# Gate and up strips as pairs in seven block products, activations through DRAM between up and down

## The chip, the cores and the metric

The kernel runs on one core of one Trainium2 chip. TensorE (PE in the profile) multiplies, and its weight loads are shown as PEld; VectorE is DVE, ScalarE is ACT, GpSimd is POOL, and SyncE (SP) issues nearly all DMAs. PSUM is TensorE's output memory, eight banks of 512 float32 values in each of 128 partitions; SBUF is the memory in which all else is kept on the core; DRAM is the memory outside it. The metric is the device time in microseconds; several runs of a kernel give a median. The profile is one execution of its own.

## The reference

Two layers over 1024 tokens of width 1024, all in float32. Layer 0 mixes with RWKV-7, layer 1 with forgetting attention over shared keys and values; both attend to a memory of 256 rows, and each ends with the part that is changed here:

```
x = x + concat([main_out, mem_out]) @ w_out[l]
h = rms_norm(x, ffn_norm[l])
gu = h @ w_gate_up                       # 1024 -> 2 * 2816
x = x + (silu(gu[:, :2816]) * gu[:, 2816:]) @ w_down      # 2816 -> 1024
```

Between the layers the shared keys and values (`w_kv`) and layer 1's input (`b_w_in`) are projected, with an RMS norm per head on keys and queries.

## The kernel before, in words

The stream X lies transposed in SBUF, features on partitions: 8 tiles k of 128 features by 1024 tokens. A projection is a sequence of **strips**: 128 output columns of a weight, 1024 x 128 values in 8 tiles. SyncE loads a strip into one of three raw buffers (L199, `load_strip`). GpSimd splits it in `split_strip`: a cast gives the high part (L211), a subtraction the low part (L213), both in a ring of three strips. TensorE's `gemm_strip` (L236) then makes for each k tile three products, high x high, high weight x low h, low weight x high h, each in two halves of 512 tokens: 6 matmuls of 128 x 512 per k tile, 48 per strip, into two PSUM banks. GpSimd's cast waits until TensorE has finished the strip that held the ring's slot.

A phase is a block in which each engine runs its own list in order, and phases are separated by a barrier. In the order of time: input projection, RWKV, memory attention, `out0`, `ffn0`, the projections `kv` and `in_b`, forgetting attention, memory attention, `out1`, `ffn1`, the transposition at the end.

**phase_out_and_ffn, phase_ffn.** `out` multiplies by w_out and adds to X. `ffn` begins with ScalarE making h's high parts (L444) and VectorE the low parts (L457), one k tile after the other, for which TensorE's first strip waits; the squares for the RMS norm (L448, L463) run beside TensorE. Then 22 feature tiles f in four groups of 6, 6, 5 and 5. For each f there is a gate strip and an up strip. VectorE takes both out of PSUM times rms (L1968, L1971), ScalarE does Silu (L1956), VectorE multiplies (L1974) and the product is split again (L1959, L1977) into `act_hi` and `act_lo`. After a group come 8 down strips of 6 or 5 k tiles, whose results VectorE adds to X (L1982).

**norm_and_gemm** does `kv` and `in_b`. For a strip of heads VectorE takes the result out (L698), ScalarE squares it (L623), TensorE sums over the head in the middle of the next strip (L716, `head_sum`), ScalarE takes the root (L631), VectorE the reciprocal (L702) and the scaled result (L704). Each engine has one list, so L704 of one strip stands ahead of L698 of the next.

## Time and profile before

| | |
|---|---|
| median of 3 runs | 3237.96 us (3234.74 to 3243.04) |
| span of the profiled execution | 3239.2 us |
| PE busy | 2979.5 us, 92% of the span |
| DVE busy | 1323.6 us, 41% |
| POOL busy | 920.7 us, 28% |
| ACT busy | 638.8 us, 20% |
| DMA | 198.17 MB, mean 61 GB/s |

The profiled execution stands 1.2 us above the median and within the range of the runs. A row of a group of instructions reads: line, engine, operation, output<-inputs, shapes, count | busy time, mean ns of one | idle time of the engine just before them and what ended it. Matmuls overlap in the pipe, so the 390 ns of one is not its price; the distance from one to the next is.

### The profile page before, as it was taken

To read this page: it belongs to the slowest core of one execution; us is meant where nothing else is said; L and a number is where in the kernel's file an instruction comes from. 1 tells how busy PE (TensorE), PEld (TensorE's weight loads), DVE (VectorE), ACT (ScalarE), POOL (GpSimd) and SP (SyncE) were. 2 spreads that over 40 slices of the span, in tenths; PEclk is the share of its full clock that TensorE was granted. 3 is DMA by queue.
4 is the path that set the end of the run, shared out by engine and by line. 5 is a ranking of instruction groups with operands and counts; after the bars stand their busy time and mean duration, and the time that the engine had idled before them with its cause. 6 is when DMAs were issued, how large, how long until landed. Compare 5 with 4: busy or idle time off the path is not lost. (4 is left out here: it accounts for less than half of the span.)

```text
span 3239.2 us, 53681 instructions
## 1 busy us (share of the span) xinstructions
PE 2979.5 (92%) x23833; PEld 2394.5 (74%) x23833; DVE 1323.6 (41%) x1722; ACT 638.8 (20%) x1032; POOL 920.7 (28%) x640
## 2 busy tenths in 40 slices
PE   7999588888689999999999989979879999999998
PEld 6888367677567888888887667746557888888887
DVE  6334256665334312222235646647732422313132
ACT  4111333343222100000002122135431200101000
POOL 4342123333212333232323222211003333333321
PEclk9999599999699999999999989989989999999999
DMA  6332200000121111111212222222121111121211
GB/s 203 93 112 69 78 23 23 23 23 4 41 92 46 46 53 46 46 52 38 61 35 95 85 72 65 85 108 101 40 97 47 44 47 53 40 59 36 62 36 69
DMA packets 236269, 198.17 MB, mean 61 GB/s; under 512 B 7494, under 2 KB 219580, under 8 KB 234760
## 3 DMA queue, kind: packets, MB, share of 16 engines
q1 hardware_dynamic: 235288, 194.08, 19.1%
q8 instruction: 189, 3.10, 0.4%
q10 hardware_dynamic: 272, 0.63, 0.1%
q14 instruction: 40, 0.33, 0.0%
q0 software_dynamic: 480, 0.03, 0.0%
HBM read 155.35 MB, written 39.37 MB: 60 GB/s over the span
## 5 line engine op out<-in xcount | busy, mean ns | idle before, releaser
L211 POOL CAST w_hi_b<-w_raw_b 128x1024 fp32r<-128x1024 f32 (+2 forms) x195 | 188.0, 964 | 1518.8 <-PE ps L236 1356.4
L236 PE MATMUL ps<-h_hi_f,w_hi_b 128*128 128x512 f32 x1664 | 516.6, 392 | 18.1 <-DVE h_lo_f L1897 9.1
L236 PE MATMUL ps<-h_lo_f,w_hi_b 128*128 128x512 f32 x1664 | 515.2, 391 | 0.0
L236 PE MATMUL ps<-h_hi_f,w_lo_b 128*128 128x512 f32 x1664 | 514.4, 390 | 0.0
L213 POOL TENSOR_TENSOR w_lo_b<-w_raw_b,w_hi_b 128x1024 fp32r<-128x1024 f32 (+2 forms) x195 | 430.5, 2208 | 15.6
L236 PEld LDWEIGHTS ps<-h_hi_f,w_hi_b 128*128 128x128 f32 x1664 | 313.3, 189 | 86.6 <-issue 18.1
L236 PEld LDWEIGHTS ps<-h_lo_f,w_hi_b 128*128 128x128 f32 x1664 | 314.2, 189 | 65.6
L236 PEld LDWEIGHTS ps<-h_hi_f,w_lo_b 128*128 128x128 f32 x1664 | 314.0, 189 | 65.7
L1982 DVE TENSOR_TENSOR x_res<-x_res,ps 128x1024 f32<-128x1024 f32 x64 | 78.1, 1221 | 365.0 <-PE ps L236 365.0
L236 PE MATMUL ps<-act_hi,w_hi_b 128*128 128x512 f32 x704 | 217.4, 390 | 2.5 <-DVE act_lo L1977 2.5
L236 PE MATMUL ps<-act_lo,w_hi_b 128*128 128x512 f32 x704 | 216.8, 389 | 0.0
L236 PE MATMUL ps<-act_hi,w_lo_b 128*128 128x512 f32 x704 | 216.8, 389 | 0.0
L1971 DVE TENSOR_TENSOR full_f<-ps,rms_f 128x1024 f32<-128x1024 f32 x44 | 53.9, 1224 | 395.9 <-PE ps L236 395.9
L1956 ACT ACTIVATE silu<-silu 128x1024 f32<-128x1024 f32 x44 | 46.7, 1061 | 661.3 <-DVE silu L1968 661.3
L1280 POOL TENSOR_TENSOR join<-lab,consts_sb 128x256 f32<-128x256 f32 x120 | 86.4, 743 | 304.9 <-DVE xx L1406 297.1
L236 PE MATMUL ps<-h_hi_b,w_hi_b 128*128 128x512 f32 x432 | 142.5, 411 | 20.5 <-DVE h_lo_b L457 20.5
L236 PEld LDWEIGHTS ps<-act_hi,w_hi_b 128*128 128x128 f32 x704 | 131.8, 188 | 31.4 <-DVE act_lo L1977 4.2
L236 PEld LDWEIGHTS ps<-act_lo,w_hi_b 128*128 128x128 f32 x704 | 132.2, 188 | 27.6
L236 PEld LDWEIGHTS ps<-act_hi,w_lo_b 128*128 128x128 f32 x704 | 132.2, 188 | 27.5
L1959 ACT ACTIVATE act_hi<-full_f 128x1024 fp32r<-128x1024 f32 x44 | 46.7, 1062 | 535.7 <-DVE full_f L1974 535.7
L236 PE MATMUL ps<-h_lo_b,w_hi_b 128*128 128x512 f32 x432 | 135.0, 394 | 0.0
L236 PE MATMUL ps<-h_hi_b,w_lo_b 128*128 128x512 f32 x432 | 134.5, 393 | 0.0
(307 smaller groups left out, 4713.4 us busy)
## 6 DMA issues: line engine op xcount, KB each, us to landing
w_raw_b<-in_w_gate_up SPq DMA_DIRECT2D x88, 512.0 KB, 3.9
w_raw_b<-in_w_down SPq DMA_DIRECT2D x32, 384.0 KB, 3.5
w_raw_a<-in_a_w_in SPq DMA_DIRECT2D x23, 512.0 KB, 4.7
u_dram<-evac_a SPq DMA_DIRECT2D x23, 512.0 KB, 3.0
w_raw_b<-in_w_down SPq DMA_DIRECT2D x32, 320.0 KB, 3.1
x_dram<-x_res SPq DMA_DIRECT2D x2, 4096.0 KB, 14.5
w_raw_b<-in_w_out SPq DMA_DIRECT2D x16, 512.0 KB, 7.7
x_res<-x_dram SPq DMA_DIRECT2D x2, 4096.0 KB, 12.9
```

What stands on the lines that cost most here:

```text
L211: self.nc.gpsimd.tensor_copy(self.whi[:, r, 0:tiles, :], raw).then_inc(self.w_hi, 1)
L213: self.nc.gpsimd.tensor_tensor(self.wlo[:, r, 0:tiles, :], raw, self.whi[:, r, 0:tiles, :].bitcast(F32), ALU.subtract).then_inc(self.w_lo, 1)
L236: mm = nc.tensor.matmul(bank[:, 2 * slot + j, 0:n], w[:, k, :], h[:, k, j * n:(j + 1) * n], start=(k == 0 and a == 0 and b == 0), stop=(k ...
L1280: nc.gpsimd.tensor_tensor(join[:, l - 1], lab[:], mask(f"join{l}", 4), ALU.mult).then_inc(join_done, 1)
L1956: nc.scalar.activation(silu[:, f % 2, :], silu[:, f % 2, :], ACT.Silu).then_inc(silu_done, 1)
L1959: nc.scalar.activation(ah[:, j, :], full[:, f % 2, :], ACT.Copy).then_inc(act_hi, 1)
L1971: nc.vector.tensor_tensor(full[:, f % 2, :], self.bank2(i % 3), rms[:], ALU.mult).then_inc(self.psum_free, 1)
L1982: nc.vector.tensor_tensor(self.X[:, f, :], self.X[:, f, :], self.bank2(i % 3), ALU.add).then_inc(self.psum_free, 1)
```

## The change

In `ffn`, the gate and up strips of a feature tile f become one unit, a **pair**, except for f = 0. Cut along the input features (k tiles 0 to 3 and 4 to 7) and by gate and up, the two strips are a 2 x 2 matrix of blocks A11, A12 (gate) and A21, A22 (up), and h is one of B11, B12, B21, B22 (feature halves by token halves). Eight block products become seven, each 4 k tiles x 3 = 12 matmuls of 128 x 512 (`product`), 84 for a pair instead of 96. For that:

- GpSimd forms four sums of a pair's weight blocks, 128 x 512 each, in place or in one extra buffer (L281 to L288), and seven low parts (L290); the high parts of pairs are cast by ScalarE (L302).
- VectorE forms four sums of h, 128 x 2048 each, in X and a staging buffer (L2254 to L2259), once per layer; they are split by ScalarE (L2148) and VectorE (L2227).
- The products pass through PSUM in a set order. ScalarE copies partial sums out of PSUM ("snapped"), VectorE adds further ones to them ("summed"), and TensorE goes on adding to a bank after the copy.
- X is overwritten. `out` stores each of its rows to DRAM and ScalarE then scales it by the gain in place; the token halves are read back later. The squares and their sum are made in `out`.
- All 22 activation tiles are stored to DRAM; the 32 down units follow after all pairs. Tiles come back through two staging buffers and are split into the memory of the h blocks, by then free.

Everywhere, weights are now split and released in **blocks** of half a strip (4 k tiles), with a ring of 7 blocks instead of 3 strips and 4 raw buffers instead of 3. In plain strips GpSimd still does cast and subtraction, each in two halves.

How instructions are moved, at three places. VectorE at the start of `ffn0`, before (h's low parts, the norm's sums, then the gate and up results of f = 0):

```order
716 L457 SCALAR_TENSOR_TENSOR h_lo_f<-x_res,params_sb,h_hi_f 128x1024 x8
717 L463 TENSOR_TENSOR rms_f<-silu 128x1024
718 L463 TENSOR_TENSOR rms_f<-rms_f,silu 128x1024 x6
719 L465 RECIPROCAL rms_f<-silu 128x1024
720 L1968 TENSOR_TENSOR silu<-ps,rms_f 128x1024
721 L1971 TENSOR_TENSOR full_f<-ps,rms_f 128x1024
```

VectorE at the same place now (`stage` is the staging buffer, b_hi and b_lo are h's blocks):

```order
729 L2250 TENSOR_TENSOR b_lo<-x_res,b_hi 128x2x512 x8
730 L2252 RECIPROCAL tokens<-tokens 128x8
731 L2254 TENSOR_TENSOR x_res<-x_res 128x4x512
732 L2256 TENSOR_TENSOR stage<-x_res 128x2048
733 L2258 TENSOR_TENSOR x_res<-x_res,stage 128x4x512
734 L2259 TENSOR_TENSOR x_res<-x_res,stage 128x4x512
735 L2227 TENSOR_TENSOR b_lo<-stage,b_hi 128x2048
736 L2227 TENSOR_TENSOR b_lo<-x_res,b_hi 128x2048 x2
737 L2235 TENSOR_TENSOR x_res<-x_res,ps 128x2x512
738 L2227 TENSOR_TENSOR b_lo<-x_res,b_hi 128x2048
```

Seven operations of 128 x 2048 stand ahead of the first result's scaling (L2235), and one more behind it. ScalarE there now (L2148 with input ps copies out of PSUM, L2158 is Silu of f = 0, row 338 is the first copy of pair 1):

```order
329 L2148 ACTIVATE x_res<-ps 128x2x512
330 L302 ACTIVATE w_hi_b<-w_raw_b 128x512 x2
331 L2148 ACTIVATE b_hi<-stage 128x2048
332 L2148 ACTIVATE b_hi<-x_res 128x2048 x2
333 L2148 ACTIVATE x_res<-ps 128x2x512
334 L302 ACTIVATE w_hi_b<-w_raw_b 128x512 x2
335 L2148 ACTIVATE b_hi<-x_res 128x2048
336 L2158 ACT_TABLE_LOAD
337 L2158 ACTIVATE x_res<-x_res 128x2x512
338 L2148 ACTIVATE x_res<-ps 128x512
```

The copy of pair 1 stands behind all splits of h's sums and behind the Silu of f = 0. SyncE's queue from the last pair to the first down units, now:

```order
157 L242 DMA w_raw_b<-in_w_down 128x6x128 x2
158 L2108 DMA act_dram<-x_res 256x1x512
159 L2114 DMA stage<-act_dram 128x1024 x4
160 L2129 DMA x_res<-x_dram 128x4x512
161 L2108 DMA act_dram<-x_res 256x1x512
162 L2133 DMA x_res<-x_dram 128x4x512
163 L242 DMA w_raw_b<-in_w_down 128x6x128
164 L2114 DMA stage<-act_dram 128x1024
```

Before, there was nothing but weight loads at this place. Now tile 6 (row 164) is loaded behind the return of X and the store of the last activation tile, and VectorE splits it before it adds the first down result:

```order
868 L2242 TENSOR_TENSOR x_res<-x_res 128x2x512
869 L2246 TENSOR_TENSOR b_lo<-stage,b_hi 128x1024
870 L2296 TENSOR_TENSOR x_res<-x_res,ps 128x1024
871 L2246 TENSOR_TENSOR b_lo<-stage,b_hi 128x1024
872 L2296 TENSOR_TENSOR x_res<-x_res,ps 128x1024
```

L2242 is the product silu(gate) x up of the last f, L2246 a tile's low part, L2296 the addition to X. The diff, cut to its core:

```diff
-RING = 3
+RAW = 4
+RING = 7
+HK = KT // 2
...
+        def unit(kind, *sources):
+            first = len(self.block_at)
+            tiles = sources[0][1]
+            sizes = [HK] * 7 if kind == "pair" else [(tiles + 1) // 2, tiles // 2]
+            at = len(self.strips)
+            for source in sources:
+                self.strips.append((*source, first + len(sizes)))
+            self.block_at += [(len(self.units), b) for b in range(len(sizes))]
+            self.units.append(Unit(kind, list(range(at, len(self.strips))), sizes, first, self.pairs))
+            self.pairs += kind == "pair"
...
+            for f in range(FT):
+                gate, up = (self.strip(i["w_gate_up"][l], 0, KT, o + f * P) for o in (0, D_FF))
+                if f == 0:
+                    unit("plain", gate)
+                    unit("plain", up)
+                else:
+                    unit("pair", gate, up)
...
-        if s >= RING:
-            sp.wait_ge(self.w_lo, s - RING + 1)
-        n = self.w_raw[s % RING]
-        sp.dma_start(self.raw[:, s % RING, 0:tiles, 0:cols], src).then_inc(n, 16)
...
+        if s >= RAW:
+            sp.wait_ge(self.w_lo, self.strips[s - RAW][3])
+        sp.dma_start(self.raw[:, s % RAW, 0:tiles, 0:cols], src).then_inc(self.w_raw[s % RAW], 16)
...
+        return (first[:, 0:HK, :], first[:, HK:KT, :], self.s2[:], second[:, 0:HK, :],
+                first[:, 0:HK, :], first[:, HK:KT, :], second[:, HK:KT, :])[b]
...
+            if b == 0:
...
+            if j >= RING:
+                pool.wait_ge(self.block_done, j - RING + 1)
+            nc.gpsimd.tensor_copy(self.whi[:, r, 0:n, :], source).then_inc(self.w_hi, 1)
+            pool.wait_ge(self.w_hi, self.plain_upto[j + 1])
+        else:
+            a11, a12, s2, s1, s3, s4, a22 = (self.block_source(unit.first + i) for i in range(7))
+            formed = 4 * unit.pair
+            if b == 0:
...
+                pool.wait_ge(self.w_lo, j)
+                nc.gpsimd.tensor_tensor(s1, s1, a22, ALU.add).then_inc(self.w_sum, 1)
+                pool.wait_ge(self.w_sum, formed + 1)
+                nc.gpsimd.tensor_tensor(s2, s1, a11, ALU.subtract).then_inc(self.w_sum, 1)
+            if b == 2:
+                pool.wait_ge(self.w_sum, formed + 2)
+                pool.wait_ge(self.w_lo, j)
+                nc.gpsimd.tensor_tensor(s3, s2, a22, ALU.subtract).then_inc(self.w_sum, 1)
+                nc.gpsimd.tensor_tensor(s4, s4, s2, ALU.subtract).then_inc(self.w_sum, 1)
+            pool.wait_ge(self.w_cast, j + 1 - self.plain_upto[j])
+        nc.gpsimd.tensor_tensor(self.wlo[:, r, 0:n, :], source, self.whi[:, r, 0:n, :].bitcast(F32), ALU.subtract).then_inc(self.w_lo, 1)
...
+        if b in (0, 1, 6):
+            self.raw_wait(act, unit.strips[b // 6])
+        else:
+            act.wait_ge(self.w_sum, 4 * unit.pair + (None, None, 2, 1, 3, 4)[b])
+        if j >= RING:
+            act.wait_ge(self.block_done, j - RING + 1)
+        self.nc.scalar.activation(self.whi[:, j % RING, :, :], self.block_source(j), ACT.Copy).then_inc(self.w_cast, 1)
...
+    def product(self, pe, j, bank, block, start, stop):
+        pe.wait_ge(self.w_lo, j + 1)
+        r = j % RING
+        for k in range(HK):
+            for a, w in enumerate((self.whi, self.wlo)):
+                for h in (self.bh, self.bl)[:2 - a]:
+                    mm = self.nc.tensor.matmul(self.ps[:, bank, :], w[:, r, k, :], h[:, block, k, :],
+                                               start=(start and k == 0 and a == 0 and h is self.bh),
+                                               stop=(stop and k == HK - 1 and a == 1), skip_group_check=True)
+        mm.then_inc(self.block_done, 1)
...
+                            sp.wait_ge(self.psum_free, i)
+                            sp.dma_start(self.x_dram[:, i - 1, :], self.X[:, i - 1, :]).then_inc(kept[i - 1], 16)
...
+                        nc.scalar.activation(sq[:, k % 2, :], self.X[:, k, :], ACT.Square).then_inc(self.squared, 1)
+                        act.wait_ge(kept[k], 16)
+                        nc.scalar.activation(self.X[:, k, :], self.X[:, k, :], ACT.Copy, scale=self.param(f"ffn_norm{l}", k))
...
+                def load_tile(t):
+                    sp.wait_ge(act_stored[t % 2], 16 * (t // 2 + 1))
+                    if t >= 2:
+                        sp.wait_ge(act_lo, t - 1)
+                    sp.dma_start(staged(t), self.act_dram[t]).then_inc(act_in[t % 2], 16)
...
+                sp.wait_ge(act_full, FT)
+                sp.dma_start(X[:, HK:KT, H2], self.x_dram[:, HK:KT, H2]).then_inc(x_gate, 16)
+                store(FT - 1)
+                for f in (FT - 2, FT - 1):
+                    sp.wait_ge(act_stored[f % 2], 16 * (f // 2 + 1))
+                sp.dma_start(X[:, 0:HK, H2], self.x_dram[:, 0:HK, H2]).then_inc(x_up, 16)
+                for g in range(G):
+                    for i in range(KT):
+                        load_upto(d0 + KT * g + i + 4)
+                        if g + 1 < G and i < groups[g + 1][1]:
+                            load_tile(groups[g + 1][0] + i)
...
+                copy(gate(0), ps[:, 0:2, :]).then_inc(snapped, 1)
+                for i in range(3, 5):
+                    self.cast_block(act, first(1) + i)
+                for n in range(3):
+                    cast_sum(n)
+                act.wait_ge(self.block_done, self.done(u0 + 1))
+                act.wait_ge(t_lo, 2)
+                copy(up(0), ps[:, 3:5, :]).then_inc(snapped, 1)
+                for i in range(5, 7):
+                    self.cast_block(act, first(1) + i)
+                cast_sum(3)
+                silu(0)
...
+                    act.wait_ge(self.block_done, j + 1)
+                    if f >= 2:
+                        act.wait_ge(act_full, f - 1)
+                    copy(gate(f)[:, 0, :], ps[:, b, :]).then_inc(snapped, 1)
+                    ahead(0, 1)
+                    act.wait_ge(self.block_done, j + 3)
+                    copy(gate(f)[:, 1, :], ps[:, b, :]).then_inc(snapped, 1)
+                    ahead(2) if f + 1 < FT else ahead(2, 3)
+                    act.wait_ge(self.block_done, j + 4)
+                    act.wait_ge(t_lo, 2)
+                    if f >= 2:
+                        act.wait_ge(act_stored[f % 2], 16 * (f // 2))
+                    copy(up(f)[:, 1, :], ps[:, b + 1, :]).then_inc(snapped, 1)
+                    ahead(3, 4, 5) if f + 1 < FT else ahead(4, 5)
+                    silu(f)
+                    act.wait_ge(self.block_done, j + 7)
+                    copy(up(f)[:, 0, :], ps[:, b, :]).then_inc(snapped, 1)
+                    ahead(6)
...
+                tt(T1, T1, T3, ALU.subtract).then_inc(t_formed, 1)
+                dve.wait_ge(t_formed, 1)
+                tt(T2, X[:, HK:KT, H2], T1, ALU.subtract).then_inc(t_formed, 1)
+                dve.wait_ge(t_formed, 2)
+                tt(T3, T3, T2, ALU.subtract).then_inc(t_formed, 1)
+                tt(T4, T4, T2, ALU.subtract).then_inc(t_formed, 1)
+                for n in range(3):
+                    sum_rest(n)
+                scale_gate(0)
+                sum_rest(3)
+                scale_up(0)
...
+                            tile_rest(groups[g + 1][0] + i)
+                        n = KT * g + i
+                        if n == 0:
+                            dve.wait_ge(x_gate, 16)
+                        if n == HK:
+                            dve.wait_ge(x_up, 16)
+                        if g:
+                            dve.wait_ge(self.psum_free, n)
+                        dve.wait_ge(self.block_done, self.done(d0 + n))
+                        at = base(FT + 1 + n)
+                        tt(two(X[:, c, :]), two(X[:, c, :]), ps[:, at:at + 2, :], ALU.add).then_inc(self.psum_free, 1)
...
+                    self.product(pe, j, b, 0, True, False)
+                    self.product(pe, j + 1, b + 2, 1, True, True)
+                    pe.wait_ge(t_lo, 1)
+                    pe.wait_ge(snapped, snaps(f) + 1)
+                    self.product(pe, j + 2, b, 2, False, False)
+                    pe.wait_ge(t_lo, 2)
+                    self.product(pe, j + 3, b + 1, 3, True, False)
+                    pe.wait_ge(t_lo, 3)
+                    pe.wait_ge(snapped, snaps(f) + 2)
+                    self.product(pe, j + 4, b, 4, False, False)
+                    pe.wait_ge(snapped, snaps(f) + 3)
+                    self.product(pe, j + 5, b + 1, 5, False, True)
+                    pe.wait_ge(t_lo, 4)
+                    pe.wait_ge(summed, 3 * (f - 1) + 2)
+                    self.product(pe, j + 6, b, 6, False, True)
```

## Rows read from the trace of the kernel before

**Rows 1.** The page: busy us (share of the span) of each engine.

```profile
PE 2979.5 (92%) x23833; PEld 2394.5 (74%) x23833; DVE 1323.6 (41%) x1722; ACT 638.8 (20%) x1032; POOL 920.7 (28%) x640
```

**Rows 2.** Busy time by stretch: ends of start, us, each engine's busy us (instructions), PEclk.

```profile
1012.00:1016.00 4.00, 0.75 (x2) 0.68 (x3) 2.52 (x3) 3.36 (x4) 3.05 (x2) 0.86 0.51 144
...
2525.00:3223.00 698.00, 696.75 (x3072) 576.03 (x3070) 192.72 (x120) 48.92 (x46) 214.95 (x143) 1.00 0.15 45
```

**Rows 3.** Who TensorE waited for, 1016 to 1739 us: us, times, longest.

```profile
PE ps L236 <- DVE h_lo_f L457: 4.5, 2, 4.2
PE ps L236 <- DVE act_lo L1977: 1.2, 2, 0.6
```

**Rows 4.** Timeline of TensorE, 149 us: matmuls 256 wide into one bank.

```profile
149.24 0.28 PE L236 MATMUL ps<-mem_hi,w_hi_a 128*128 128x256 f32 x1
149.36 0.28 PE L236 MATMUL ps<-mem_lo,w_hi_a 128*128 128x256 f32 x1
```

**Rows 5.** Groups of instructions by shape, GpSimd, whole span.

```profile
L1283 POOL TENSOR_TENSOR xx<-xx,consts_sb 128x512 f32<-128x512 f32 x24 | 30.5, 1270 | 0.0
...
L211 POOL CAST w_hi_b<-w_raw_b 128x640 fp32r<-128x640 f32 x32 | 23.0, 718 | 190.0 <-PE ps L236 190.0
```

**Rows 6.** Groups by shape: ScalarE 880 to 920 us, VectorE 880 to 960 us.

```profile
L1825 ACT ACTIVATE mem_prob_t<-ps 128x512 f32<-128x512 f32 x8 | 4.8, 595 | 2.0 <-PE ps L1797 2.0
...
L1897 DVE TENSOR_TENSOR h_lo_f<-x_res,h_hi_f 128x1024 fp32r<-128x1024 f32 x8 | 9.2, 1221 | 1.4 <-ACT h_hi_f L1890 1.4
...
L1856 DVE TENSOR_TENSOR x_res<-ps,mem_scale 128x512 f32<-128x512 f32 x4 | 2.8, 692 | 4.4 <-ACT mem_scale L1831 4.4
```

**Rows 7.** DMA issues, whole span: KB each, median us to landing.

```profile
w_raw_b<-in_w_down SPq DMA_DIRECT2D x32, 384.0 KB, 3.5
...
u_dram<-evac_a SPq DMA_DIRECT2D x23, 512.0 KB, 3.0
...
x_res<-x_dram SPq DMA_DIRECT2D x2, 4096.0 KB, 12.9
...
mem_q<-u_dram SPq DMA_DIRECT2D x4, 512.0 KB, 3.9
```

**Rows 8.** Timeline at the start of `ffn0`: start us, us, what [idle before <-releaser].

```profile
1015.25 1.19 PE L236 MATMUL ps<-h_hi_f,w_hi_b 128*128 128x512 f32 x2 [4.17 <-DVE h_lo_f L457]
...
1016.25 1.05 PE L236 MATMUL ps<-h_lo_f,w_hi_b 128*128 128x512 f32 x2
...
1019.06 0.63 PE L236 MATMUL ps<-h_lo_f,w_hi_b 128*128 128x512 f32 x2
```

**Rows 9.** Timeline, VectorE and GpSimd at 1085 and 1528 us.

```profile
1085.71 2.39 POOL L213 TENSOR_TENSOR w_lo_b<-w_raw_b,w_hi_b 128x1024 fp32r<-128x1024 f32 x1
1085.75 3.43 DVE L1974 TENSOR_TENSOR full_f<-full_f,silu 128x1024 f32<-128x1024 f32 x1
...
1527.48 1.22 DVE L1982 TENSOR_TENSOR x_res<-x_res,ps 128x1024 f32<-128x1024 f32 x1 [1.76 <-PE ps L236]
...
1528.38 1.57 POOL L213 TENSOR_TENSOR w_lo_b<-w_raw_b,w_hi_b 128x640 fp32r<-128x640 f32 x1
```

**Rows 10.** Timeline of `in_b`, one strip of heads.

```profile
2005.62 6.55 DVE L702 RECIPROCAL sq_in_b<-sq_in_b 128x1024 f32<-128x1024 f32 x1 [4.31 <-ACT sq_in_b L631]
...
2010.05 1.04 POOL L211 CAST w_hi_b<-w_raw_b 128x1024 fp32r<-128x1024 f32 x1 [10.96 <-PE ps L236]
...
2011.17 2.40 POOL L213 TENSOR_TENSOR w_lo_b<-w_raw_b,w_hi_b 128x1024 fp32r<-128x1024 f32 x1
...
2012.21 2.44 DVE L704 SCALAR_TENSOR_TENSOR evac_in_b<-evac_in_b,params_sb,sq_in_b 128x1024 f32<-128x1024 f32 x1
```

**Rows 11.** TensorE's waits, `kv` 1780 to 1875 us, `in_b` 1975 to 2075 us.

```profile
PE ps L716 <- ACT sq_kv L623: 6.3, 4, 1.6
PE ps L716 <- ACT evac_kv L628: 1.7, 1, 1.7
...
PE ps L716 <- ACT sq_in_b L623: 11.0, 7, 1.6
```

487 lines of the change are left out of this document (329 added, 158 removed).

## The prediction

> **What bounds the kernel now.** I read the page first: TensorE is busy for 92% of the span, the next engine for 41% [rows 1]. A mean over stages says little, so next I read busy time by stretch. In `ffn1` from 2525 to 3223 us TensorE is busy for 696.75 of 698 us, at a granted clock of 1.00 (2.4 GHz), with 3072 matmuls [rows 2]. That gives 698 / 3072 = 0.227 us from one matmul to the next, and this, not the 390 ns of one record, is the price of a matmul. Then the waits: from 1016 to 1739 us, nearly all of `ffn0`, TensorE waited 4.5 us for h's first low parts and 1.2 us for activations [rows 3]. So the two ffn stages are bound by the number of matmuls, and a matmul removed there is 0.227 us of the kernel as long as each other engine and each wait keeps up. Two other places matter because the change passes through them: the loop over head strips in `kv` and `in_b`, in which TensorE does wait [rows 11], and the phase borders.
>
> **What is removed.** A pair has 84 matmuls instead of 96. With 21 pairs and two layers, 2 x 21 x 12 = 504 go: 504 x 0.227 = 114.4 us. Two doubts on the price. First, the 12 matmuls of a product go into one bank one after the other, where two banks alternated. Matmuls of 256 columns into one bank stand 0.12 us apart [rows 4]; 256 columns at 2.4 GHz are 0.107, and 512 are 0.213 against the 0.227 paid, so the surplus is 0.013 in both and one bank costs nothing. Second, there are seven borders with waits in a pair instead of two. The old borders cost nothing (696.75 of 698 us holds over all strips), so I take none if what is waited for is in time.
>
> **Is it in time within a pair?** TensorE takes 12 x 0.227 = 2.72 us per product, 19.05 us per pair. GpSimd now has 4 sums and 7 low parts of 128 x 512: 11 x 1.27 [rows 5], with 0.08 between them (the gap between cast and subtraction) 14.9 us. ScalarE has 7 casts and 4 copies out of PSUM at about 0.6 [rows 6] and a Silu of 1.1: 7.7 us. VectorE has 3 additions from PSUM at 0.69, two scalings and a product at 1.22 [rows 6]: 5.7 us. None is the bound. The order matters more. After product 1 ScalarE copies its bank (0.6) while TensorE does product 2 (2.72), and TensorE adds to that bank only in product 3. The copies after products 3 and 4 likewise have one product of cover. The ring of seven lets block i of the next pair be split when TensorE has left block i of this one, so it has six products, 16 us, to get ready. I take zero for the pairs; the cover ends when one link is 2 us late.
>
> **The price of sharing between VectorE and GpSimd.** At 1085.75 a VectorE product of two SBUF inputs started 0.04 us after a GpSimd subtraction and took 3.43 us instead of 1.22; GpSimd ended at 1088.10, and 1.08 us later VectorE did. At 1527.48 an addition with one input from PSUM ran beside GpSimd's work at its normal 1.22, and GpSimd kept its 1.57 [rows 9]. So two-SBUF-input operations and GpSimd's take turns, whole instructions at a time. The Trainium skill says this too ("SBUF — State Buffer", section "SBUF: two separate sides": an exclusive lock, held by whichever starts first for the whole instruction); the trace agrees. By the page's neighbouring remark that VectorE's own pair never waits, one could expect no stretch; with 3.43 against 1.22 the measurement decides. This enters twice, once as a gain and once as a loss.
>
> **Gain in the head loops.** In `in_b` the chain of one head strip is: reciprocal 6.55, scaled result L704 2.44, then the next result out of PSUM, the square, the head sum on TensorE, the root [rows 10]. L704 starts at 2012.21 while GpSimd is in its subtraction (2011.17 to 2013.57), so it takes 2.44 instead of some 1.2. Now GpSimd splits half a strip when a strip is done: a cast of at most 0.72 (the 640-wide one) and 1.27 [rows 5]. From 2010.05 that ends at 2012.12 at the latest, before L704 begins. The other half comes half a strip later, when VectorE has nothing of two SBUF inputs to do. So each round loses 1.2 us, and TensorE has the idle time for it: it waits 1.6 us per round, 7 rounds in `in_b` and 4 + 1 in `kv` [rows 11]. 12 x 1.2 = 14 us. From below 0 (if the halves fall on L704 after all; the margin is 0.1 us), from above 12 x 1.57 = 19.
>
> **Losses, per layer.**
> *End of `out`: +4.2.* The last row of X must be stored (3.0 to landing for 512 KB [rows 7]), then ScalarE scales it (1.06, twice the 0.6 less its start), before the barrier. Nothing hides it: TensorE is done. The start of `out0` has one GpSimd block beside h's first low part, +1 in that layer only.
> *Start of `ffn`: +11.* Take 0 at the barrier. As before, h's low parts follow each other at 1.2 and TensorE starts after about 2.6 (1012.6 to 1015.25 [rows 8]) and ends its first plain strip at 15.5 and the second at 27.5; products 1 and 2 of pair 1 end at 33. Product 3 waits for the first copy of pair 1, which in ScalarE's list stands behind all splits of h's sums and the Silu of f = 0. That chain: low parts until 13.9, with two of GpSimd's between them; four sums of 128 x 2048 at 2.3 (twice 1.22 less the start), each with a GpSimd operation of 1.27 in between: 28; three low parts at 2.3 and two more of GpSimd's: 38; scaling 39; ScalarE meanwhile copies up(0) and makes the fourth cast until 40; table 1.3, Silu 1.1, copy 0.6: 43. TensorE idles 43 - 33 = 10. Without taking turns the same chain ends at 35 and costs 2. After an idle stretch the clock is low: at the start of `ffn0` the granted clock is 0.86 over 4 us and two matmuls take 1.05 us against 0.63 later [rows 2, 8], the level being 1.2 GHz; I add 2. The old stage had 1.9 us of matmuls for the norm's sums where the new has 1: -1. Sum 11; bounds 1 and 14.
> *Last pair: +1.5.* Tiles 2 and 3 can be loaded only when 0 and 1 have been split, and ScalarE waits for tile 3 ahead of the copy after product 4. Product 2 ends at 5.4, addition and two low parts until 8.7, load 3.9 [rows 7] 12.6, cast 13.7, copy 14.3; TensorE wants it at 13.6. With turns 15 to 16. Bounds 0 and 3.
> *Start of down: +12.* With 0 at the last pair's start, the pair ends at 20.5. Tiles 4 and 5 hold VectorE until 21 to 23 by the same chain, then come addition, scaling, Silu, copy, scaling, product: the last activation at 28 to 29. Then SyncE reads back half of X's second half (1 MB), stores the tile, waits for it, reads the other 1 MB, a weight strip and tile 6. From 512 KB in 3.0 and 4096 KB in 12.9 [rows 7] a queue moves 1 MB in 2.8 us after 1.6: the store lands at about 28.5 + 6.2 = 34.7, tile 6 at 34.7 + 7.4 = 42, cast and low part 44.5, addition 45.7. VectorE's first addition to X stands behind tile 6, and the third down unit waits for it. Two units of 36 matmuls last 16.4, so TensorE is ready at 36.9: idle 9 to 10, and 2 for the clock. Bounds 5 and 18.
> Behind it each unit of 8.2 us covers a tile load, a cast and a low part; the DMA traffic added (22 tiles of 0.5 MB out and back, X out and back, some 31 MB a layer) is small beside 698 us.
>
> **Sum.** -114.4 - 14 + 2 x (4.2 + 11 + 1.5 + 12) + 1 = -70. The profiled execution has 3239.2; 3239.2 - 70 = 3169, and since that execution was 1.2 above the median, the median should be 3168.
>
> **The rivals.**
> *The stages' starts are cheap.* If VectorE and GpSimd get past each other in the long operations and the DMAs are quick, the ffn start costs 2 and the down start 6: 3168 - 2 x 15 = 3138. For it: the low bound of each chain. Against: the 3.43 us of L1974.
> *The head loops give nothing.* A margin of 0.1 us is thin; then 3182.
> *The starts cost more.* 18 at down, 14 at the ffn start and 3 in the last pair: 3168 + 2 x 10.5 = 3189.
> *A pair is not set by TensorE.* GpSimd's list is the only one near 19.05. If VectorE's additions with a PSUM input took turns too (against rows 9), or each of the 11 operations waited for one of VectorE's of 0.69, GpSimd would need 11 x (1.35 + 0.69) = 22.4 us per pair, and the ring would pass that on: 42 x 3.4 = +143, 3311. It decides from 20.7 us per pair on: there 42 x 1.66 eats the whole 70, and beyond it the kernel is slower.
> *The change doesn't save what it says,* because one link is late in each pair by about a microsecond (a copy, or the act_full wait ahead of it): 42 us back, 3210.
>
> **How the numbers follow.** Forecast 3168 with 0.50; cheap starts 0.15; no gain in the loops 0.11; dearer starts 0.11; a microsecond late in each pair 0.07; pairs bound elsewhere 0.06. The range 3136 to 3204 takes in the first four and leaves out the last two. What can be told from no change is about 0.3%, 10 us. Faster 0.92; same 0.03, from late links of 1.5 us; slower 0.05.
>
> **What would show it right or wrong.** Right: 84 matmuls of a pair in 19.1 us with no TensorE wait from pair 3 to 20; L704 at 1.2 to 1.3 in `kv` and `in_b` and rounds of 13.3 us; one wait of about 10 us on ScalarE's copy in pair 1; one of about 10 us on L2296 in the third down unit, ended by a chain from tile 6's load. Wrong: TensorE waits on `snapped` or on w_lo in the middle of the pairs, or GpSimd busy all through a pair; then the forecast fails at its largest term.

## The result, and the profile after

The changed kernel takes 3162.32 us (median of 4 runs, 3158.38 to 3166.96) beside 3237.68 for the kernel before on the same chip (4 runs, 3234.74 to 3243.04): a ratio of 0.9761, 95% interval 0.9745 to 0.9778. The forecast was 3168, its range 3136 to 3204. The profiled execution has a span of 3156.3 us (3239.2 before), so it is one of the shorter ones of its kernel, as medians of 4 allow; its difference of 82.9 is 7.5 more than that of the medians, and the sum below is held against the medians.

The page after, busy us of each engine, against [rows 1]:

```profile
PE 2873.3 (91%) x23385; PEld 2311.5 (73%) x23385; DVE 1356.4 (43%) x1864; ACT 933.0 (30%) x1522; POOL 1344.4 (43%) x1218
```

TensorE has lost 106 us of busy time. GpSimd has gained 424 and ScalarE 294, and over the whole span neither is near a bound.

Busy time by stretch (ends, us, busy us of PE, PEld, DVE, ACT, POOL with instructions, PEclk, DMA share, GB/s), against [rows 2]: end of product 2 of pair 1 and the idle time behind it, the 4.5 us after that, pairs 2 to 20 of `ffn0`, pairs of `ffn1`, the restart in down:

```profile
1051.00:1055.30 4.30, 0.21 (x1) 0.00 (x0) 3.64 (x3) 4.27 (x5) 4.13 (x3) 1.00 0.19 51
1055.30:1059.80 4.50, 4.41 (x12) 3.51 (x13) 2.85 (x3) 1.02 (x2) 4.42 (x3) 0.62 0.91 266
...
1070.70:1432.40 361.70, 361.70 (x1597) 299.53 (x1596) 117.59 (x114) 138.92 (x229) 280.67 (x209) 1.00 0.30 91
2500.00:2866.00 366.00, 366.00 (x1616) 303.08 (x1615) 119.49 (x116) 139.86 (x230) 283.57 (x212) 1.00 0.30 90
...
1481.20:1485.20 4.00, 3.94 (x9) 3.14 (x10) 3.06 (x4) 1.06 (x1) 0.32 (x1) 0.50 0.98 289
```

Nineteen pairs in 361.7 us are 19.04 us each, TensorE is busy for all of it, and GpSimd for 280.7 / 19 = 14.8 us a pair. The two restarts show a granted clock of 0.62 and 0.50, as means over the stretch: 12 matmuls take 4.4 us instead of 2.7, 9 take 4.0 instead of 2.0.

TensorE's waits from 1016 to 1711 us (us, times, longest), the whole of `ffn0`, against [rows 3]:

```profile
PE ps L324 <- DVE x_res L2296: 11.5, 1, 11.5
PE ps L2302 <- PEq L1990: 5.4, 1, 5.4
PE ps L352 <- DVE b_lo L2227: 4.2, 1, 4.2
PE ps L352 <- ACT x_res L2148: 1.5, 1, 1.5
```

These four are all. In order of time they are the barrier at the start (`PEq` is TensorE's sequencer), pair 1, the last pair, and the start of down. In `ffn1` the same ones are 5.3, 4.4, 1.8 and 10.9.

The end of `out0`, where X's last row is stored and scaled before the barrier opens (start, us, what [idle before <-releaser]):

```profile
1011.91 0.34 SPq L2006 DMA_DIRECT2D x_dram<-x_res  x1
...
1014.54 1.15 ACT L2025 ACTIVATE x_res<-x_res,params_sb 128x1024 f32<-128x1024 f32 x1 [1.57 <-DMA x_dram<-x_res]
```

From the store to the scaled row it is 3.8 us. At the start of `ffn0` VectorE and GpSimd work in turn; VectorE first, then GpSimd:

```profile
1032.04 3.26 DVE L2256 TENSOR_TENSOR stage<-x_res 128x2048 f32<-128x2048 f32 x1
1035.33 3.26 DVE L2258 TENSOR_TENSOR x_res<-x_res,stage 128x2048 f32<-128x2048 f32 x1
```
```profile
1033.11 3.33 POOL L288 TENSOR_TENSOR w_raw_b<-w_raw_b,w_sum_b 128x512 f32<-128x512 f32 x1
1036.40 3.33 POOL L290 TENSOR_TENSOR w_lo_b<-w_sum_b,w_hi_b 128x512 fp32r<-128x512 f32 x1
```

GpSimd's 128x512 operation shows 3.33 us instead of the 1.27 of [rows 5]: most of it is waiting for its turn. ScalarE at the same place:

```profile
1048.57 1.03 ACT L2148 ACTIVATE x_res<-ps 128x1024 f32<-128x1024 f32 x1 [5.70 <-PE ps L352]
1049.49 1.14 ACT L302 ACTIVATE w_hi_b<-w_raw_b 128x512 fp32r<-128x512 f32 x2
1050.53 1.90 ACT L2148 ACTIVATE b_hi<-x_res 128x2048 fp32r<-128x2048 f32 x1
1052.45 1.28 ACT L2158 ACT_TABLE_LOAD   x1
1053.74 1.06 ACT L2158 ACTIVATE x_res<-x_res 128x1024 f32<-128x1024 f32 x1
1054.71 0.58 ACT L2148 ACTIVATE x_res<-ps 128x512 f32<-128x512 f32 x1
```

The first row is the copy of up(0), the last the first copy of pair 1, which ends at 1055.29. TensorE's product 3 follows; beside it the operation of VectorE that the table of waits names:

```profile
1055.39 0.68 PE L352 MATMUL ps<-b_hi,w_hi_b 128*128 128x512 f32 x1 [4.18 <-DVE b_lo L2227]
```
```profile
1052.46 2.73 DVE L2227 TENSOR_TENSOR b_lo<-x_res,b_hi 128x2048 fp32r<-128x2048 f32 x1 [0.66 <-ACT b_hi L2148]
```

VectorE's `b_lo` ends at 1055.19, 0.1 us before the copy, but it is the fourth low part, which product 3 doesn't use. What product 3 needs is the copy.

Start of down; SyncE, then ScalarE, then VectorE:

```profile
1461.54 0.53 SPq L2108 DMA_DIRECT2D act_dram<-x_res  x1
1468.74 0.37 SPq L2133 DMA_DIRECT2D x_res<-x_dram  x1
...
1469.76 0.49 SPq L2114 DMA_DIRECT2D stage<-act_dram  x1
```
```profile
1477.24 1.06 ACT L2148 ACTIVATE b_hi<-stage 128x1024 fp32r<-128x1024 f32 x1 [18.67 <-DMA stage<-act_dram]
```
```profile
1478.40 1.68 DVE L2246 TENSOR_TENSOR b_lo<-stage,b_hi 128x1024 fp32r<-128x1024 f32 x1 [17.32 <-ACT b_hi L2148]
1480.00 1.21 DVE L2296 TENSOR_TENSOR x_res<-x_res,ps 128x1024 f32<-128x1024 f32 x1
```

That is the chain of the forecast: last activation stored at 1461.54, tile 6 asked for at 1469.76, cast, low part, and only then the first addition to X, at whose end (1481.21) TensorE goes on. One strip of heads in `in_b`, against [rows 10]:

```profile
1983.49 0.61 POOL L272 CAST w_hi_b<-w_raw_b 128x512 fp32r<-128x512 f32 x1 [6.00 <-PE ps L324]
1984.18 1.29 POOL L290 TENSOR_TENSOR w_lo_b<-w_raw_b,w_hi_b 128x512 fp32r<-128x512 f32 x1
1985.66 1.28 DVE L823 SCALAR_TENSOR_TENSOR evac_in_b<-evac_in_b,params_sb,sq_in_b 128x1024 f32<-128x1024 f32 x1
```

GpSimd's half-strip is done 0.19 us before the scaled result starts, which takes 1.28 instead of 2.44. A round is 13.34 us (14.48 before), and TensorE waits 0.46 us in it instead of 1.6 [rows 11].

### The profile page after: what moved, and what is told of

It reads as the page before. It is cut to its first block and busy times, and to the rows that moved or that the text cites. A ratio compares the mean times of both kernels' runs of the same rounds, so it can differ in the third digit from the quotient of the medians.

```text
span 3156.3 us, 54822 instructions
## 1 busy us (share of the span) xinstructions
PE 2873.3 (91%) x23385; PEld 2311.5 (73%) x23385; DVE 1356.4 (43%) x1864; ACT 933.0 (30%) x1522; POOL 1344.4 (43%) x1218
## 5 line engine op out<-in xcount | busy, mean ns | idle before, releaser
L290 POOL TENSOR_TENSOR w_lo_b<-w_raw_b,w_hi_b 128x512 fp32r<-128x512 f32 (+1 forms) x474 | 582.7, 1234 | 191.7 <-ACT w_hi_b L302 173.9
L272 POOL CAST w_hi_b<-w_raw_b 128x384 fp32r<-128x384 f32 (+1 forms) x222 | 129.8, 585 | 803.4 <-PE ps L324 589.3
L352 PE MATMUL ps<-b_hi,w_hi_b 128*128 128x512 f32 x1176 | 459.3, 391 | 11.8 <-DVE b_lo L2227 8.6
L352 PE MATMUL ps<-b_lo,w_hi_b 128*128 128x512 f32 x1176 | 458.7, 390 | 0.0
L352 PE MATMUL ps<-b_hi,w_lo_b 128*128 128x512 f32 x1176 | 458.5, 390 | 0.0
L352 PEld LDWEIGHTS ps<-b_hi,w_hi_b 128*128 128x128 f32 x1176 | 221.4, 188 | 59.5 <-DVE b_lo L2227 9.3
L324 PE MATMUL ps<-b_hi,w_hi_b 128*128 128x512 f32 x768 | 240.8, 395 | 22.4 <-DVE x_res L2296 22.4
L352 PEld LDWEIGHTS ps<-b_hi,w_lo_b 128*128 128x128 f32 x1176 | 221.4, 188 | 46.3
L352 PEld LDWEIGHTS ps<-b_lo,w_hi_b 128*128 128x128 f32 x1176 | 221.6, 188 | 45.8
L324 PE MATMUL ps<-b_lo,w_hi_b 128*128 128x512 f32 x768 | 239.8, 394 | 0.0
L324 PE MATMUL ps<-b_hi,w_lo_b 128*128 128x512 f32 x768 | 239.0, 393 | 0.0
L2296 DVE TENSOR_TENSOR x_res<-x_res,ps 128x1024 f32<-128x1024 f32 x64 | 78.1, 1221 | 332.0 <-PE ps L324 332.0
L302 ACT ACTIVATE w_hi_b<-w_raw_b 128x512 fp32r<-128x512 f32 x252 | 157.3, 627 | 213.4 <-PE ps L352 213.4
L324 PEld LDWEIGHTS ps<-b_hi,w_hi_b 128*128 128x128 f32 x768 | 146.0, 191 | 53.4 <-DVE x_res L2296 23.3
L2148 ACT ACTIVATE x_res<-ps 128x512 f32<-128x512 f32 (+1 forms) x172 | 103.8, 603 | 238.6 <-PE ps L352 215.7
L324 PEld LDWEIGHTS ps<-b_lo,w_hi_b 128*128 128x128 f32 x768 | 146.4, 191 | 30.9
L324 PEld LDWEIGHTS ps<-b_hi,w_lo_b 128*128 128x128 f32 x768 | 146.1, 190 | 30.8
L2148 ACT ACTIVATE b_hi<-stage 128x1024 fp32r<-128x1024 f32 (+1 forms) x46 | 49.8, 1095 | 303.4 <-DMA stage<-act_dram 152.8
## 6 DMA issues: line engine op xcount, KB each, us to landing
x_dram<-x_res SPq DMA_DIRECT2D x2, 4096.0 KB, 14.4
```

What stands on the lines that cost most here:

```text
L272: nc.gpsimd.tensor_copy(self.whi[:, r, 0:n, :], source).then_inc(self.w_hi, 1)
L290: nc.gpsimd.tensor_tensor(self.wlo[:, r, 0:n, :], source, self.whi[:, r, 0:n, :].bitcast(F32), ALU.subtract).then_inc(self.w_lo, 1)
L302: self.nc.scalar.activation(self.whi[:, j % RING, :, :], self.block_source(j), ACT.Copy).then_inc(self.w_cast, 1)
L324: mm = nc.tensor.matmul(bank[:, banks + part, 0:n], w[:, j % RING, i, :], operand(lo, k, part), start=(k == 0 and a == 0 and lo == 0), sto ...
L352: mm = self.nc.tensor.matmul(self.ps[:, bank, :], w[:, r, k, :], h[:, block, k, :], start=(start and k == 0 and a == 0 and h is self.bh), ...
L2148: copy = lambda out, x: nc.scalar.activation(out, x, ACT.Copy)
```

## The experiments

All of them are edits of the changed kernel. Times are medians; the ratio is to the kernel before on the same chip, whose medians lie between 3237.7 and 3241.8 us on the chips used. A difference of a few us between kernels measured on different chips therefore shows nothing by itself. The changed kernel itself has 0.9761 [0.9745, 0.9778].

| | us | ratio, 95% interval |
|---|---|---|
| eight products | 3264.37 | 1.0074 [1.0059, 1.0089] |
| GpSimd, four more a pair | 3243.58 | 1.0011 [1.0002, 1.0020] |
| GpSimd, seven more a pair | 3408.95 | 1.0517 [1.0500, 1.0534] |
| whole strips, early | 3161.39 | 0.9751 [0.9738, 0.9765] |
| whole strips, late | 3166.95 | 0.9774 [0.9761, 0.9787] |
| whole strips, late, one instruction | 3178.57 | 0.9812 [0.9795, 0.9829] |
| GpSimd held at ffn's start | 3159.90 | 0.9751 [0.9738, 0.9764] |
| copy first in pair 1 | 3151.97 | 0.9722 [0.9709, 0.9735] |
| row waited for in ffn | 3156.81 | 0.9739 [0.9725, 0.9753] |
| addition first in down | 3136.07 | 0.9676 [0.9663, 0.9690] |
| copy, addition, row together | 3120.55 | 0.9629 [0.9616, 0.9642] |
| the same, tile 3 behind the copy | 3119.27 | 0.9631 [0.9617, 0.9646] |

### What a product is worth, and what the rest costs

```
-                    self.product(pe, j + 1, b + 2, 1, True, True)
+                    self.product(pe, j + 1, b + 2, 1, True, True, twice=True)
...
```

With `twice`, `product` runs its 12 matmuls two times, and the second pass overwrites the first.

> Product 2 of every pair is multiplied twice, the first pass being overwritten, so that a pair has eight block products in TensorE's time (96 matmuls of 512 columns and not 84) with everything else of the change in place. Theory (the saving is TensorE's 504 matmuls at 0.227 us and the pairs are bound by TensorE alone): a pair lasts 21.76 and not 19.04 us, the program 3162 + 42 x 2.72 = 3276, that is about 38 us above the kernel before: the price of everything else in the change. Rival (something other than TensorE sets part of the pairs' time, so the eighth product is partly hidden): clearly under 3276, down to 3240.

Pairs 2 to 20 of both layers last 21.76 us, as the theory has it. Most of them lie in this stretch:

```profile
1070.40:1477.70 407.30, 407.30 (x1798) 337.25 (x1798) 114.74 (x112) 136.39 (x224) 277.86 (x207) 1.00 0.26 80
```

The time is 3264, 12 under the 3276 expected. In pair 1 TensorE waited anyway, so there the extra product is hidden in part: pair 1 lasts 23.9 and 23.6 us where 25.1 + 2.7 = 27.8 would be the sum, 8 us in all; the last pairs hide another 0.8. That leaves 3 us of the 12 unexplained. With eight products the kernel is 23 us slower than before (1.0074), where 38 were expected: what else the change does is a cost, and the product saved pays for it.

### When GpSimd becomes the bound

```
             pool.wait_ge(self.w_cast, j + 1 - self.plain_upto[j])
+            nc.gpsimd.tensor_tensor(self.wlo[:, r, 0:n, :], source, self.whi[:, r, 0:n, :].bitcast(F32), ALU.subtract).then_inc(self.w_again, 1)
+            pool.wait_ge(self.w_again, j + 1 - self.plain_upto[j])
...
```

The second kernel has the two new lines under `if b % 2 == 0`, with a count to match. A pair has 4 sums and 7 subtractions on GpSimd, 11 operations; the first kernel makes 18 of them and the second 15. (The expectation of the first says 9 and 18 subtractions; they are 7 and 14, and GpSimd's busy time in the changed kernel is 14.8 us a pair, not 13.)

> GpSimd makes every low part of the pairs' blocks twice (18 subtractions of 128x512 a pair and not 9); the result is unchanged. In the kernel as it is GpSimd works some 13 of a pair's 19.04 us. Theory by the rival that named a bound of 20.7 us a pair: about 12 more us of GpSimd make it the bound, a pair lasts 24 to 26 us, the program 3162 + 42 x 5 to 7 = 3370 to 3450. Other theory (the second subtractions fit in GpSimd's free time and only VectorE's wide steps are slowed): a pair stays at 19.04 to 20 us, under 3200.

> GpSimd makes the low parts of the pairs' blocks 0, 2, 4 and 6 twice: 15 operations of 128x512 a pair, where the kernel has 11 (14.8 us of GpSimd's time in 19.04) and the doubled one had 18 (24.5 us a pair, 1.36 per operation). Theory (a pair lasts the longer of TensorE's 19.04 us and 1.36 us per GpSimd operation): 20.4 us a pair, 3162 + 42 x 1.4 = 3220. Rival (the order of links and the waits between engines lengthen the pair before GpSimd is full, since its second subtractions delay S3, S4 and the casts behind them): 21 us and more, over 3245.

Stretch 1100 to 1430 us of the kernel with seven more, and of that with four more:

```profile
1100.00:1430.00 330.00, 282.72 (x1132) 227.43 (x1131) 82.24 (x82) 98.64 (x163) 317.33 (x241) 0.92 0.23 69
```
```profile
1100.00:1430.00 330.00, 308.88 (x1341) 250.08 (x1340) 97.08 (x96) 115.11 (x192) 318.72 (x241) 1.00 0.28 83
```

GpSimd is busy for 96 and 97% of it. With 18 operations a pair lasts 24.7 us on average, with 15 it lasts 20.69, 1.37 and 1.38 us an operation. So a pair lasts the longer of TensorE's 19.04 and some 1.38 us per GpSimd operation. The 11 of the kernel as it is make 15 of 19, which by this estimate leaves room for two more.

The expectation of 3220 was 23 too low, and some 18 of that are in the last pairs, which last 30.9 and 31.5 us (20.8 and 21.2 in the changed kernel). GpSimd, SyncE and ScalarE in the last pair of `ffn0`, which starts at 1466.6:

```profile
1478.34 1.29 POOL L293 TENSOR_TENSOR w_lo_b<-w_raw_b,w_hi_b 128x512 fp32r<-128x512 f32 x1
```
```profile
1479.66 0.97 SPq L242 DMA_DIRECT2D w_raw_b<-in_w_down  x2
...
1481.33 9.73 SPq L2118 DMA_DIRECT2D stage<-act_dram  x4
```
```profile
1487.09 1.06 ACT L2152 ACTIVATE b_hi<-stage 128x1024 fp32r<-128x1024 f32 x1 [11.54 <-DMA stage<-act_dram]
```

The first strips of down need a raw buffer that GpSimd gives back with its last low part of the pair (until 1479.63). The loads of the activation tiles stand behind these strips in SyncE's queue, ScalarE waits 11.5 us for one of them ahead of its copy, and TensorE 9.6 us for the copy. In the changed kernel SyncE comes to these strips 3 us after the last pair's start, and here after 13. So a late GpSimd costs more at this border than in the pairs. The other theory is missed as well: its 21 us a pair did not come, and 3243.6 is just under its 3245.

### The head rounds: where, or how long

```
...
+        pool.wait_ge(self.block_done, j + 1 - RING + 1)
+        for i in (j, j + 1):
+            nc.gpsimd.tensor_copy(self.whi[:, i % RING, 0:n, :], self.block_source(i)).then_inc(self.w_hi, 1)
+        pool.wait_ge(self.w_hi, self.plain_upto[j + 2])
+        for i in (j, j + 1):
+            nc.gpsimd.tensor_tensor(self.wlo[:, i % RING, 0:n, :], self.block_source(i), ...
```

GpSimd makes both casts of a strip and then both subtractions, once both slots of the ring are free. (What the expectation calls VectorE's column sum is the scaled result, L823 in the changed kernel.)

> Undoes one part: in kv and in_b GpSimd splits a whole strip again (both halves once both slots are free), as the kernel before did; the pairs stay. Theory (the half-strip split is what took the 1.14 us out of each head round, since VectorE's column sum no longer meets GpSimd's subtraction): the 12 rounds go from 13.34 back to about 14.48 us, TensorE's gap per round from 0.47 to about 1.6, the program to 3162 + 12 x 1.14 = 3176. Rival (the granularity of the split is irrelevant, something else in the change shortened the rounds): rounds stay at 13.34 and the time at 3162.

The rival's numbers came: 3161 us, rounds of 13.34. My theory as written was wrong, that half a strip instead of a whole one is what counts. The rows show why (VectorE, then GpSimd):

```profile
1984.43 1.28 DVE L841 SCALAR_TENSOR_TENSOR evac_in_b<-evac_in_b,params_sb,sq_in_b 128x1024 f32<-128x1024 f32 x1
```
```profile
1988.96 2.52 POOL L305 TENSOR_TENSOR w_lo_b<-w_raw_b,w_hi_b 128x512 fp32r<-128x512 f32 x2
```

With the ring of seven, whole strips can go half a strip earlier than before, and GpSimd's subtractions lie 4.5 us behind the scaled result. So the place had moved with the size. The next kernel has the old place. Its one change against this one:

```
-        pool.wait_ge(self.block_done, j + 1 - RING + 1)
+        pool.wait_ge(self.block_done, j + 2 - RING + 1)
```

> As the whole-strip kernel before it, but GpSimd waits for both halves of the strip three back, which is the kernel before's condition; the first whole-strip kernel waited for its first half only, so its subtractions began one half strip earlier, and its rounds stayed at 13.34 us. Theory now (it is the place of GpSimd's work in the round, not its size, that decides whether it meets VectorE's scaled result): casts start 2.2 us ahead of that operation, the two subtractions of 1.27 lie on it, and it ends 0.4 us late if VectorE gets its turn between them, 1.7 us late if not: rounds of 13.7 to 14.6 us and 3167 to 3178, in the middle of what the kernel before had if it is 14.48. Rival (the rounds got shorter by something else): 13.34 and 3162.

```profile
1984.86 3.52 POOL L305 TENSOR_TENSOR w_lo_b<-w_raw_b,w_hi_b 128x512 fp32r<-128x512 f32 x2
```
```profile
1985.79 1.44 DVE L841 SCALAR_TENSOR_TENSOR evac_in_b<-evac_in_b,params_sb,sq_in_b 128x1024 f32<-128x1024 f32 x1
```

They meet, but VectorE gets its turn between the two subtractions and loses 0.16 us, and rounds are 13.50. Neither theory gives that: the new one had 13.7 to 14.6, the rival 13.34, and 0.16 x 12 is 2 us. What is left is the length of the one instruction that VectorE meets:

```
+        if r + 1 < RING and unit.sizes == [HK, HK]:
...
+            nc.gpsimd.tensor_copy(self.whi[:, r:r + 2, :, :], raw).then_inc(self.w_hi, 2)
...
+            nc.gpsimd.tensor_tensor(self.wlo[:, r:r + 2, :, :], raw, self.whi[:, r:r + 2, :, :].bitcast(F32), ALU.subtract).then_inc(self.w_lo, 2)
```

> As the kernel before this one (whole strips, released by the second half of the strip three back, rounds of 13.50 us), but one cast and one subtraction of 128x1024 per strip where the two slots are neighbours in the ring (6 strips of 7), and two of 128x512 where not. Theory (VectorE waits for the rest of the one GpSimd instruction it meets, and the kernel before lost 1.14 us a round because that instruction was 2.4 us long; two of half the length let VectorE in between): rounds of about 14.4 us where the strip goes in one instruction, some 10 of 12, with the scaled result at about 2.4 us, 3172 to 3175. Rival (the seven-slot ring or the earlier loads shortened the rounds): 13.5 us stay, and 3165.

```profile
2006.31 2.38 POOL L304 TENSOR_TENSOR w_lo_b<-w_raw_b,w_hi_b 128x1024 fp32r<-128x1024 f32 x1
2007.27 2.52 DVE L848 SCALAR_TENSOR_TENSOR evac_in_b<-evac_in_b,params_sb,sq_in_b 128x1024 f32<-128x1024 f32 x1
```

Of the twelve rounds the two with split instructions stay at 13.5 us. The ten others are longer. Eight last 14.57. One, just behind a round with split instructions, lasts 14.87: there VectorE comes sooner, 0.65 us after GpSimd's start (1991.74), and its result takes 2.82. The first of `kv`, which has 14.30 in the changed kernel, lasts 15.55. TensorE is idle for 1.7 to 2.0 in a long round. The time is 11.6 us above the kernel with two instructions at the same place; the expected 3172 to 3175 was 4 to 7 too low, as the rounds were to have 14.4. But for the round of 14.87, VectorE comes 0.9 to 1.0 us after the start of a subtraction in both kernels, so only the subtraction's length differs. That settles it: the loss in the kernel before was a 2.4 us GpSimd instruction that lay on VectorE's; either a shorter instruction or another place takes it away, and the change did both.

The rows give more than that. The scaled result takes 1.28 us alone. It lost 1.16 us where 1.36 of GpSimd's instruction was left when it came (the kernel before, [rows 10]), 1.24 where 1.42 was left, 1.54 where 1.74 was left, and 0.16 where 0.36 was left (whole strips, late: the first of the two subtractions takes 1.29 and ends at 1986.15). Each time the loss is what was left, less 0.2 us. A short instruction therefore bounds the loss and doesn't remove it: had VectorE come at the start of one of 1.29 us, it would have lost some 1.1, an estimate by the same difference.

### The start of ffn

```
+                if unit.pair % (FT - 1) == 0:
+                    pool.wait_ge(self.hold, 3)
...
+            self.hold = t_lo
...
-                for i in range(3, 5):
-                    self.cast_block(act, first(1) + i)
+                self.cast_block(act, first(1) + 3)
...
```

The first lines are GpSimd's, ahead of the third sum of pair 1's weights (`s3`). `t_lo` counts VectorE's low parts of h's sums. ScalarE casts block 4 later, with 5 and 6.

> At the first pair of each layer GpSimd waits for VectorE's first three tile low parts before it makes its own operand sums, and ScalarE casts block 4 behind the copy of up(0). Theory of turns (VectorE's 128x2048 operations last 3.3 us at ffn's start because they take turns with GpSimd's): those beside a resting GpSimd fall to about 2.1 us, low parts are there earlier, the 4.2 and 1.7 us of pair 1 mostly go, about 6 us a layer, 3150. Rival (3.3 us is the operation's own price): they stay at 3.3, and TensorE waits for GpSimd's late low parts instead, 3162 to 3175.

VectorE at the start of `ffn0` of this kernel, GpSimd's first operation after its rest, and ScalarE's first copy of pair 1:

```profile
1032.29 2.29 DVE L2258 TENSOR_TENSOR stage<-x_res 128x2048 f32<-128x2048 f32 x1
...
1041.23 4.49 DVE L2229 TENSOR_TENSOR b_lo<-x_res,b_hi 128x2048 fp32r<-128x2048 f32 x2
```
```profile
1045.89 1.30 POOL L289 TENSOR_TENSOR w_raw_b<-w_sum_b,w_raw_b 128x512 f32<-128x512 f32 x1 [15.78 <-DVE b_lo L2229]
```
```profile
1053.71 0.58 ACT L2151 ACTIVATE x_res<-ps 128x512 f32<-128x512 f32 x1
```

The turns are shown: with GpSimd at rest the same operations take 2.29 us instead of 3.26 to 3.38, and the third low part is done at 1045.7 instead of 1050.7. But the time is 3160 and not the expected 3150: ScalarE now waits for GpSimd's late sums, its copy comes only 1.0 us earlier, and pair 1 lasts 23.9 and 24.0 instead of 25.1. The 5 us were handed on.

```
                 copy(up(0), ps[:, 3:5, :]).then_inc(snapped, 1)
+                act.wait_ge(self.block_done, first(1) + 1)
+                copy(gate(1)[:, 0, :], ps[:, base(2), :]).then_inc(snapped, 1)
                 for i in range(5, 7):
                     self.cast_block(act, first(1) + i)
...
```

> Changes the order on ScalarE at the first pairs: its first copy of pair 1 stands right behind the copy of up(0), ahead of the casts of blocks 5 and 6, the sum's cast and the silu of strip 0; in the later pairs it stands ahead of the silu too. Theory (the 4.2 and 4.4 us gaps before product 3 of pair 1 are ScalarE's queue ahead of that copy): both gaps go, and part of the 1.7 us of colder clock with them, 5 to 6 us a layer, so about 3152. Rival (the copy is next to VectorE's low parts of the tiles and t_lo, which end just as late): the gap moves to the next product and less than 1 us a layer is won, 3160 to 3162.

```profile
1050.25 1.51 ACT L2148 ACTIVATE x_res<-ps 128x1024 f32<-128x1024 f32 x2 [5.73 <-DVE b_lo L2229]
```
```profile
PE ps L352 <- issue: 0.8, 1, 0.8
PE ps L352 <- ACT x_res L2148: 0.2, 1, 0.2
```

Both copies now run together at 1050.25, product 3 follows product 2 at once, and what is left in `ffn0` are two waits of 1.0 us together. Pair 1 lasts 20.6 and 20.2 us, and the time is 3152 as expected. VectorE's order was not touched, so this also shows that the copy was what TensorE waited for, although the table of waits had named VectorE.

### The end of out

```
-                        act.wait_ge(kept[k], 16)
+                        if k < KT - 1:
+                            act.wait_ge(kept[k], 16)
...
                 for k in range(KT):
+                    if k == KT - 1:
+                        act.wait_ge(self.kept_last, 16 * (l + 1))
+                        nc.scalar.activation(X[:, k, :], X[:, k, :], ACT.Copy, scale=self.param(f"ffn_norm{l}", k)).then_inc(self.squared, 1)
...
```

> Moves one wait: the store of X's last row is waited for, and the row scaled, within ffn rather than ahead of the barrier at the end of out. Theory (the 3.8 us that out's end grew by are that store's landing plus the scale): 3.5 us a layer come back, about 3155. Rival (ffn's first instructions on ScalarE need the row just as soon, or TensorE has its own wait for tile data there): the gap appears a few us later in ffn and the time stays within 1 us of 3162.

```profile
1012.08 1.22 DVE L2042 TENSOR_TENSOR stage<-stage,sq_o 128x1024 f32<-128x1024 f32 x1 [1.12 <-ACT sq_o L2024]
```

Of the 3.5 us only 1.4 came back at the barrier (TensorE's idle time goes from 5.36 to 3.93 in both layers): the row is no longer last, but VectorE's addition of the last square is, until 1013.30. The rest is not the barrier: pair 1 is 3.0 us shorter in `ffn0` and 1.0 longer in `ffn1`. Why is not shown, and pair 1 of `ffn0` isn't steady anyway: it lasts 26.8 us instead of 25.1 in two other kernels in which nothing of it was changed (the addition first in down, and whole strips in one instruction). The time fell by 5.5, the spans of the profiled executions by 2.3, and the intervals of the two ratios overlap (0.9739 and 0.9761). How much of that is the edit stays open.

### The start of down, and all together

```
-                        if g + 1 < G and i < groups[g + 1][1]:
-                            tile_rest(groups[g + 1][0] + i)
+                        if g + 1 < G and 0 <= i - 2 < groups[g + 1][1]:
+                            tile_rest(groups[g + 1][0] + i - 2)
```

> Changes the order on VectorE at down's start: the first two adds to X of a group stand ahead of the next group's tile low parts. Theory (the 11.5 and 10.9 us gaps at down's start are the chain load of tile 6, cast, low part, first add, bank free): the first add no longer waits for tile 6, the gap and the 2 us of colder clock behind it go, about 12 us a layer, so about 3137. Rival (the add next waits for its own operand: the gate product's load lands at about 1467 in the kernel as it is, or the next group's matmuls wait for the tile's low part instead): a gap of 3 to 6 us stays, and the time is 3145 to 3155.

Stretch from the start of down to its end in `ffn0`, and VectorE there:

```profile
1457.10:1690.00 232.90, 232.90 (x1029) 192.85 (x1028) 65.60 (x52) 18.79 (x19) 93.18 (x125) 1.00 0.35 102
```
```profile
1471.32 1.22 DVE L2296 TENSOR_TENSOR x_res<-x_res,ps 128x1024 f32<-128x1024 f32 x1 [6.38 <-DMA x_res<-x_dram]
```

TensorE has no idle time left in the stage, and the clock stays at 1.00. The rival's wait exists, VectorE waits for X until 1471.32, but the addition ends at 1472.54 and the third down unit wants its bank at 1457.1 + 16.4 = 1473.5: it fits by 1 us. Expected 3137, measured 3136.

> Three edits together: ScalarE's copy of pair 1 first, VectorE's adds ahead of the tile low parts at down's start, X's last row waited for within ffn. Theory (each of the three starts is a chain of its own, so they add): about 10 + 24 + 7 us under 3162, 3120 to 3125. Rival (a shared limit, such as the loads or VectorE's queue, is only handed from one to the next): 3140 to 3155.

The time is 3120.55. The three edits alone give 10.4, 26.3 and 5.5 us, 42.1 together; all at once give 41.8. By the ratios, which take out the chips, it is 47 and 43, so the agreement to 0.3 us is luck, but within a few us they add, and each start is a chain of its own. One term of the forecast is then left, the last pair:

```
-                    ahead(2) if f + 1 < FT else ahead(2, 3)
+                    ahead(2)
-                    ahead(3, 4, 5) if f + 1 < FT else ahead(4, 5)
+                    ahead(3, 4, 5)
...
```

VectorE's low part of tile 3 moves behind its second addition in the same way.

> The kernel with the three starts changed, and in the last pair ScalarE's copy after product 4 stands ahead of the cast of tile 3 (VectorE's low part of tile 3 behind its second addition). Theory (the 1.3 to 1.8 us by which the last pair is longer than the others are the load of tile 3, for which ScalarE waits ahead of that copy): the last pair goes from 20.7 to 19.04 us, 1.7 us a layer, 3117 against 3120.6. Rival (tile 3 comes later, and with it tiles 4 and 5, the activations of the last pair and down's start): the 1.7 us come back in the down stage, 3120 to 3123.

All waits of TensorE from 1010 to 1690 us in this kernel:

```profile
PE ps L2310 <- PEq L1991: 3.9, 1, 3.9
PE ps L352 <- ACT x_res L2150: 1.2, 1, 1.2
PE ps L324 <- DVE x_res L2304: 0.6, 1, 0.6
PE ps L352 <- issue: 0.2, 1, 0.2
```

The last pair lasts 19.04 us in both layers (20.66 and 20.84 without the edit), and 0.6 and 0.4 us of the 1.7 come back as a wait in down. So the cause was that ScalarE waited for tile 3 ahead of the copy. The profiled spans differ by 4.1 us, the medians by 1.3 with overlapping intervals (ratios 0.9631 and 0.9629): the trace shows the step, the times don't resolve it. These two kernels are 1.3% faster than the changed one (0.963 against 0.9761).

## Why the prediction was right

| step | forecast, us | measured, us |
|---|---|---|
| 504 matmuls | -114.4 | -114.2 (42 x 2.72) |
| other costs within pairs 2 to 20 | 0 | 0 (19.04 each) |
| head rounds | -14 | -13.7 (12 x 1.14) |
| end of `out`, a layer | +4.2 | +3.8 |
| start of `ffn`, a layer | +11 | +8.0, +7.2 |
| last pair, a layer | +1.5 | +1.8, +2.1 |
| start of down, a layer | +12 | +13.5, +12.9 (wait and clock) |
| start of `out` | +1 | +1 in each layer |
| sum | -70 | -73 (medians: -75) |

**The pairs.** The large term stands on three readings that all held: 0.227 us a matmul also with twelve into one bank [rows 4], no cost at the borders of products, and GpSimd at 14.8 us a pair where 14.9 was worked out from [rows 5]. The eighth product put back takes 2.72 us in each of the pairs 2 to 20. The slow rival's figure, that nothing is gained from 20.7 us a pair on, came out with four more operations (20.69 us, ratio 1.0011), but partly by luck. The pairs 2 to 20 account for 38 x 1.65 = 63 us of the loss there, and another 20 lie in the last pairs, which the forecast's 42 x 1.66 = 70 doesn't have. Without these 20 the kernel would stand some 17 us below the kernel before, an estimate.

**The head rounds.** The size came out, and the mechanism as stated (a shorter instruction that ends before L704 begins, by a margin of 0.1 us; it was 0.19) is what the rows show. A missed margin would have cost less than the forecast held: where short instructions lay on VectorE's, with 0.36 us of the first left, 0.16 us a round was lost and not 1.2. Only where VectorE came right at the start of a short instruction would nearly all of the gain go (some 1.1 us, by the estimate above). The forecast had not seen this, and whether its chance of 0.11 was right can't be told: no run here has VectorE come early on a short instruction.

**The start of ffn** is the term with the largest error, 11 for 8.0 and 7.2. Counted from the barrier, pair 1 of `ffn0` was to end at 58.6 us and ends at 54.7. TensorE came to pair 1 2.2 us later than forecast (29.7 instead of 27.5), and ScalarE's copy ended at 39.3 instead of 43. What failed is "each with a GpSimd operation of 1.27 in between": 2.3 + 1.27 = 3.6 us for each of the wide operations, where a turn of both took 3.28. Besides, h's low parts were done at 12.7 instead of 13.9. The two shifts, TensorE's later and the copy's earlier, shrank the idle time from 10 to 4.2, where the forecast's sign of being right was a wait of about 10. The chain itself was the right one: taking its last link out of ScalarE's order takes the wait away, and resting GpSimd shortens VectorE's part of it and moves the wait on.

**End of out, last pair, start of down** hold within 1.5 us a layer, but at down two errors offset each other. From the start of the last pair the chain ended at 48.8 us and not at 45.7: the store had landed 7.2 us after its issue and tile 6 some 8.5 later, for 6.2 and 7.4 in the forecast. (Its own rule, 1.6 us and 2.8 per MB, gives 5.8 and 6.9, so the sums written there are not its rule's either.) On the other side, the kernel before had losses in down that the forecast put at nothing: its four down groups last 241.3 us a layer, and their 1056 matmuls at 0.227 would be 239.4. Against these groups the stage has grown by 11.8 and 11.2. The row at the end of `out` (ready at 1015.69) has a neighbour only 1.5 us less late (VectorE's last square, as the experiment showed), which the forecast did not name: as a term of the sum it was right, as a thing to win it is worth 1.4.

**What is left.** The sum with the measured terms is -73 against -75.4 by the medians. That the forecast's -70 is so near owes something to luck: its 11 at the start of `ffn` was too much, its 12 at down and 1.5 in the last pair too little. In the two profiled executions the stages that the table covers are 76 us shorter: 31.3 and 33.2 from the last matmul of `out` to the first one behind the layer, 13.8 in `kv` and `in_b`, less 2 at the starts of `out`. Most of the 3 us beyond the table are the losses of the kernel before in down. The other 6.5 of the 82.9 us lie where the argument has nothing to say, and their cause is not traced: 1.4 ahead of `out0`, 2.4 in forgetting attention and its neighbours, 2.7 in `out1`.

## What to carry to other kernels

Price a change of the number of matmuls by the distance between their starts in a stretch in which nothing waits, and the rest of the change by the borders of its stages: here the steady part was exact, and the some 53 us of loss in `ffn` lay in four places a layer. At such a place look at what stands in the late engine's list ahead of the instruction that TensorE waits for, and move the wait that isn't needed yet behind it: three such moves gave back 42 of them. A list that is off the critical path counts at a border too: with four more operations a pair GpSimd gave its buffers back 10 us later, and through SyncE's queue that cost 10 us in the last pair. And before moving one, find the next-late engine: it decides whether the gain is 13 us, as in down, or 1.4, as at the end of `out`.

## What the hardware showed unexpectedly

When VectorE and GpSimd take turns, what is left of the one GpSimd instruction that it meets is what VectorE loses (less 0.2 us in the four cases here), and not GpSimd's amount of work: met at the same place, the same 1024 columns cost it 0.16 us a round in two instructions of 1.29 us, and 1.24 us in one of 2.38. Where both have a queue of such work, both show the duration of a full turn (3.26 to 3.38 us for operations that take 2.29 and 1.27 alone). Of a busy share in such a stretch some three fifths are waiting on GpSimd and three tenths on VectorE. The granted clock stayed at 1.00 after an idle time of 1.5 us in the last pair (matmuls 0.23 apart from the second on), and stood at 0.62 and 0.50 over the 4 to 4.5 us behind idle times of 4.2 and 11.5 us, which cost 1.7 and 2.0 us beside the wait itself.
